# Two layers of modulation, a 31-tap convolution and its norm spread over the engines of one core

## What is computed

```python
cond = silu(c)
mod = cond @ ada_w[l] + ada_b[l]              # l = 0, 1; 1024 x 3072 each
shift, scale, gate = split(mod, 3)
h = rms_norm(x, norm_g[l]) * (1 + scale) + shift
z = h @ even_w_in                             # 1024 x 7296
a_val, a_glu, a_gate, r, k, v, wd, ad, b_gate = split_cols(z)
u = a_val * sigmoid(a_glu)
y = depthwise_conv(u, conv_w, width 31) + conv_vec[0]
ya = silu(layer_norm(y, conv_vec[1], conv_vec[2])) * silu(a_gate)
yb = group_norm(state recurrence of r, k, v, decay, a) ... * silu(b_gate)
x = x + gate * (concat(ya, yb) @ even_w_out)
```

## Time and profile before

| | us |
|---|---|
| median of 3 runs | 2145.01 (2143.09 to 2145.21) |
| the profiled execution: its own time | 2143.33 |
| its span | 2141.6 |
| PE busy | 2029.2 (95%) |
| DVE busy | 1356.5 (63%) |
| ACT busy | 920.6 (43%) |
| POOL busy | 69.5 (3%) |

### The profile page before, as it was taken

The page is one execution under the profiler, slowest core; times in us unless marked ns, Lnnn a source line. Parts: engine busy times, 40 slices in busy tenths (PEclk is TensorE's granted clock), DMA queues, the critical chain, the costliest instruction groups (busy, mean ns, idle before and its releaser), DMA issues. The chain is left out here.

```text
span 2141.6 us, 28761 instructions
## 1 busy us (share of the span) xinstructions
PE 2029.2 (95%) x12095; PEld 1811.2 (85%) x12095; DVE 1356.5 (63%) x1667; ACT 920.6 (43%) x1062; POOL 69.5 (3%) x109
## 2 busy tenths in 40 slices
PE   4987999879999999999999989999999999999998
PEld 3876888667778786899998879999999999998976
DVE  6779758642274223666532358787879787878872
ACT  1511111112125311344433357676767676666654
POOL 2000000000000010000021000000000000000000
PEclk7989899989999999999999999999999999999999
DMA  9834421323332243255674239898989899898980
GB/s 312 282 118 144 151 80 59 120 78 107 131 118 79 79 160 114 64 158 187 191 242 140 100 139 367 313 364 315 359 316 355 320 347 338 330 348 327 353 320 21
DMA packets 225884, 452.22 MB, mean 211 GB/s; under 512 B 6976, under 2 KB 91208, under 8 KB 225752
## 3 DMA queue, kind: packets, MB, share of 16 engines
q1 hardware_dynamic: 222432, 445.44, 59.4%
q0 software_dynamic: 1632, 4.75, 0.8%
q10 hardware_dynamic: 1688, 0.15, 0.1%
HBM read 448.21 MB, written 2.10 MB: 210 GB/s over the span
## 5 line engine op out<-in xcount | busy, mean ns | idle before, releaser
L1726 DVE TENSOR_TENSOR ring_r<-ring,his_r 128x2816 fp32r<-128x2816 f32 (+1 forms) x192 | 587.1, 3087 | 57.6 <-ACT his_r L1337 57.2
L1337 ACT ACTIVATE his_r<-ring 128x2816 fp32r<-128x2816 f32 (+1 forms) x192 | 490.8, 2560 | 194.6 <-DMA ring<-in_moe_w_dram 183.1
L1023 PE MATMUL bank<-his_r,hg_r 128*128 128x352 f32 x2048 | 355.5, 326 | 0.8 <-ACT hg_r L1359 0.8
L1023 PEld LDWEIGHTS bank<-his_r,hg_r 128*128 128x128 f32 x2048 | 332.9, 188 | 2.0 <-issue 0.9
L2183 PE MATMUL bank<-hT,ring 128*128 128x256 f32 x912 | 217.0, 395 | 14.4 <-DVE arena L2726 10.8
L2183 PEld LDWEIGHTS bank<-hT,ring 128*128 128x128 f32 x912 | 176.3, 197 | 43.2 <-issue 18.3
L1023 PE MATMUL bank<-ring_r,hg_r 128*128 128x352 f32 x1024 | 186.1, 324 | 0.0
L1967 PE MATMUL bank<-arena,ring 128*128 128x256 f32 x800 | 178.2, 380 | 1.8 <-ACT cw L1279 0.7
L1967 PEld LDWEIGHTS bank<-arena,ring 128*128 128x128 f32 x800 | 151.4, 190 | 24.4 <-issue 1.3
L1023 PEld LDWEIGHTS bank<-ring_r,hg_r 128*128 128x128 f32 x1024 | 169.2, 188 | 0.0
L1967 PE MATMUL bank<-hT,ring 128*128 128x256 f32 x624 | 142.4, 386 | 5.8 <-ACT hT L2491 4.0
(11 more groups left out here) (492 smaller groups left out, 2541.0 us busy)
## 6 DMA issues: line engine op xcount, KB each, us to landing
ring<-in_moe_w_dram SPq DMA_DIRECT2D x128, 1408.0 KB, 8.1
ring<-in_moe_w_dram SPq DMA_DIRECT2D x48, 1536.0 KB, 8.9
ring<-in_even_w_in_dram SPq DMA_DIRECT2D x28, 1024.0 KB, 6.7
ring<-in_ada_w_dram SPq DMA_DIRECT2D x24, 1024.0 KB, 9.4
ring<-in_ffn_w_dram SPq DMA_DIRECT2D x22, 1024.0 KB, 5.4
ring<-in_odd_w_in_dram SPq DMA_DIRECT2D x9, 2048.0 KB, 7.7
ring<-in_moe_w_dram SPq DMA_DIRECT2D x16, 1024.0 KB, 6.6
ring<-in_a_w_in_dram SPq DMA_DIRECT2D x6, 2048.0 KB, 8.0
```

What stands on the lines that cost most here:

```text
L1023: ins = mm(bank[first + m][:, 0:WC], x[:, KT // 2 * late + k, :], w[:, k, WC * m:WC * m + WC], start=(not late and k == 0 and s == "hg_hi" ...
L1337: A(moe_hi(n), moe_w(n), ACT.Copy).then_inc(sem("moe_hi"), 1)
L1726: V.tensor_tensor(moe_lo(n), moe_w(n), moe_hi(n).bitcast(F32), ALU.subtract).then_inc(sem("moe_lo"), 1)
```

## The change

Five things are edited. **First**, groups 0 and 2 of the modulation go to PE: `ada_direct` takes the raw weight chunk as stationary operand and the column `cond` as moving operand, 32 matmuls of one column a group. DVE keeps the ten other groups. **Second**, the reciprocal of the first norm (L2704) stands between the halves of group 3, `kar(0)` ahead of the second val0 tile, and the DVE steps of zV tiles 0 and 1 in the inversion, at t = 29 and 31. **Third**, channel tiles 3 and 7 of the convolution leave DVE: ACT makes each tap's product (`tap_products`, 31 a tile, three buffers), POOL adds it up (60 additions). DVE keeps 186 taps, all of them done by the second chunk of `states(1)`. **Fourth**, the convolution's layer norm goes into chunks 2 and 3 of `states(1)`. **Fifth**, `eoA` starts right behind `states(1)`, and the head norm's steps stand between its tiles.

```diff
+        TAP_PART = [side[:, 3312 + T * b:3312 + T * b + T] for b in range(3)]
+        TAPS, PRE, LATE_TILES = 186, 29, (3, 7)
...
+        ADA_PE = (0, 2)
+        ADA_DVE = tuple(c for c in range(12) if c not in ADA_PE + ADA_ACT)
+        add("adaP", 4, 512, 2 * len(ADA_PE), 1, ada_src(ADA_PE), reader="ada_pe")
+        add("adaD", 4, 512, 2 * len(ADA_DVE), 1, ada_src(ADA_DVE), reader="dve")
...
             # gpsimd
+            for g, ct in enumerate(LATE_TILES):
+                for j in range(1, 31):
+                    b = 30 * g + j - 1
+                    pool.wait_ge(sem("tap_products"), 31 * g + j + 1)
+                    if b >= 1:
+                        pool.wait_ge(sem("tap_added"), b)
+                    pool.tensor_tensor(YY[:, ct, :], YY[:, ct, :], TAP_PART[b % 3], ALU.add).then_inc(sem("tap_added"), 1)
...
             # tensor
+            def ada_direct(c):
+                n = 2 * ADA_PE.index(c)
+                halves = [wait_chunk(pe, "adaP", n, 0), wait_chunk(pe, "adaP", n + 1, 0)]
+                for j in range(4):
+                    for k in range(KT):
+                        ins = mm(bank[2][:, 4 * c + j:4 * c + j + 1], halves[k // 4][:, k % 4, j * P:(j + 1) * P], cond[:, k:k + 1],
+                                 start=(k == 0), stop=(k == KT - 1))
+                ins.then_inc(sem("ada_columns"), 2)
...
             for q in range(KT):
                 norm_tile(0, q)
-            for c in range(4):
-                ada(c)
+            ada(1)
+            ada_direct(2)
+            ada(3)
...
             z("val0", 0)
-            z("val0", 1)
             pe.wait_ge(sem("rwkv_set"), 3)
             for g in range(8):
                 kar(0, g)
+            z("val0", 1)
...
+                    if tt == 1 and n == 2:
+                        pe_sum(bank[3][:, 0:T], YY, [(taps, TAPS), (sem("tap_added"), 60)], sem("mean_summed"))
+                    elif tt == 1 and n == 3:
+                        pe_sum(bank[2][:, 0:T], YSQ, [(sem("squares_ready"), 9)], sem("var_summed"))
                     fill(n, 0)
...
+            eo(0)
             pe_head_sum(bank[2][0:16, 0:T], YT, [(sem("y_ready"), 4)], sem("head_summed"))
-            pe_sum(bank[3][:, 0:T], YY, [(taps, 248)], sem("mean_summed"))
+            eo(1)
             pe_head_spread(nr[0:16, :], [(sem("gn_mean_ready"), 1)], sem("spread_ready"))
-            pe_head_sum(bank[2][0:16, 0:T], A4T_SQ, [(sem("squares_ready"), 9)], sem("head_summed"))
-            pe_sum(bank[3][:, 0:T], A3T_SQ, [(sem("squares_ready"), 10)], sem("var_summed"))
+            eo(2)
+            eo(3)
+            pe_head_sum(bank[2][0:16, 0:T], A4T_SQ, [(sem("squares_ready"), 10)], sem("head_summed"))
+            eo(4)
             pe_head_spread(nr[0:16, :], [(sem("head_norm"), 2), (sem("centred"), 5)], sem("spread_ready"))
-            for q in range(KT):
-                z("eoA", q, lambda k: YY[:, k, :], (lambda k: (sem("conv_gated"), k // 4 + 1)) if q == 0 else None)
+            for q in range(5, KT):
+                eo(q)
...
             # scalar
+                        b = 30 * g + j - 1
+                        if b >= 3:
+                            act.wait_ge(sem("tap_added"), b - 2)
+                        A(TAP_PART[b % 3], UP[:, ct, j:j + T], ACT.Copy, scale=cw[:, 8 * j + ct:8 * j + ct + 1])\
+                            .then_inc(sem("tap_products"), 1)
...
             for n in range(NC4):
                 carry(0, n)
+                tap_products(3)
+                value(4 + 2 * n) if n < 2 else glu(2 * n)
+                tap_products(3)
+                value(5 + 2 * n) if n < 2 else glu(2 * n + 1)
+                tap_products(2 if n < 3 else 1)
             act.wait_ge(sem("glu_used"), 2)
             b_gate(0)
+            tap_products(3)
             for n in range(8, 12):
                 toks_taken(n)
             b_gate(1)
+            tap_products(3)
             for n in range(12, 16):
                 toks_taken(n)
             for m in range(2, 6):
                 b_gate(m)
+                tap_products(4)
...
             # vector
+            dve.wait_ge(sem("norm_rooted"), 1)
+            step(V.reciprocal(nr[:, :], nr[:, :]))
+            ada(3, 1)
             modulation(0, 0, 16)
...
             for t in range(1, C):
+                if t in (29, 31):
+                    value(t // 31)
...
-            for q in range(KT):
-                lerp(q + 18, "zV", q, VV[:, q, :], col("mu_v", q))
-                if q < 6:
-                    ada(1, 6 + q)
+            for q in range(2, KT):
+                value(q)
+                ada(9 + (q - 2) // 2, q % 2)
...
-            conv(40)
-            states(0, 16)
+            conv(PRE)
+            states(0, lambda n, m: 8)
...
-            states(1, 16)
+            states(1, lambda n, m: (8, 8, 9)[2 * n + m] if 2 * n + m < 3 else 0)
             y_add(1)
-            conv(248)
```

More of the change, by code:

```diff
@@ L282, in z_bank, with ada_group @@
             return bank[ZTILES.index((name, q)) % 2][:, 0:T]
[L284 to L288, removed]
+        SUMMED = {c: sum(b not in ADA_PE for b in range(c + 1)) for c in range(-1, 12)}
+        def ada_group(c):
+            name, groups = next(x for x in (("adaP", ADA_PE), ("adaD", ADA_DVE), ("adaA", ADA_ACT)) if c in x[1])
+            return [(name, 2 * groups.index(c)), (name, 2 * groups.index(c) + 1)]
+        order = [x for c in range(4) for x in ada_group(c)] + [("zL", 0), ("zK", 0), *ada_group(4), ("zK", 1), *ada_group(5), ("zK", 2),
+                                                               *ada_group(6), ("zK", 3), *ada_group(7), ("zR", 0)]
+        a8 = ada_group(8)
+        order += [a8[0], ("zR", 1), a8[1], ("zR", 2), ("zR", 3), ("val0", 0), ("val0", 1), ("glu0", 0), ("glu0", 1), ("zV", 0),
+                  *ada_group(9), ("zV", 1), *ada_group(10), ("zV", 2), *ada_group(11), ("zV", 3)]
         order += [(n, j) for n in ("val1", "glu1", "zB", "zA") for j in range(phases[n]["n"])]
@@ L2610, in b_gate, with tap_products @@
                 evict("zB", m, BG[:, m, :], ACT.Silu).then_inc(acc_taken["act"], 1)
+            tap = [0]
+            def tap_products(n):
+                for m in range(tap[0], tap[0] + n):
+                    g, j = m // 31, m % 31
+                    ct = LATE_TILES[g]
+                    if j == 0:
+                        act.wait_ge(sem("glu_used"), g + 1)
+                        act.wait_ge(sem("inverse_ready"), 1)
+                        act.wait_ge(sem("ada_summed"), SUMMED[11])
+                        A(YY[:, ct, :], UP[:, ct, 0:T], ACT.Identity, bias=col("cv0", ct), scale=cw[:, ct:ct + 1]).then_inc(sem("tap_products"), 1)
+                    else:
+                        b = 30 * g + j - 1
[3 more added lines that the diff above has]
+                            .then_inc(sem("tap_products"), 1)
+                tap[0] += n
             w_taken(0)
@@ L2709, in _ @@
             dve.wait_ge(sem("cond_ready"), 1)
-            for j in range(4):
-                ada(0, j)
+            ada(1, 0)
+            ada(1, 1)
             dve.wait_ge(sem("params_taken"), 1)
@@ L2865, in states, with conv_centre, conv_scale @@
                     V.tensor_tensor(SS[:, :, :], SS[:, :, :], pe_, ALU.mult).then_inc(sem("state_ready"), 1)
-                    conv(fill // 2)
+                    conv(fill(n, 1))
+                    if tt == 1 and n == 3:
+                        conv_scale()
+            def conv_centre():
+                dve.wait_ge(sem("mean_summed"), 1)
+                mean = bank[3][:, 0:T].unsqueeze(1).to_broadcast([P, KT, T])
+                V.scalar_tensor_tensor(YY[:, :, :], mean, -1.0 / D, YY[:, :, :], ALU.mult, ALU.add).then_inc(sem("centred"), 1)
+            def conv_scale():
+                dve.wait_ge(sem("rooted"), 2)
+                step(V.reciprocal(cw[:, :], cw[:, :]))
+                dve.wait_ge(sem("centred"), 1)
+                nrb = cw[:, :].unsqueeze(1).to_broadcast([P, 4, T])
+                for g in range(2):
+                    V.tensor_tensor(YY[:, 4 * g:4 * g + 4, :], YY[:, 4 * g:4 * g + 4, :], nrb, ALU.mult).then_inc(sem("scaled"), 1)
             def y_add(tt):
```

223 lines of the change are left out of this document (124 added, 99 removed).

## The result

| | us |
|---|---|
| before: median | 2143.82 (2142.01 to 2147.40, 20 runs) |
| changed: median | 2147.62 (2143.26 to 2158.69, 20 runs) |
| ratio | 1.0018, 95% interval 1.0009 to 1.0026 |
| span of the profiled execution | 2141.6 before, 2144.3 changed |

The change costs 0.18%, where the forecast was a gain of 0.24%. The time lies outside the 2135 to 2145 that the forecast gave itself; only the wide range of 2131 to 2152 holds it, near the price of rival 1 (2147.3). The sign is the other one.

What follows compares the result with a forecast made beforehand. PE, busy 95% of the span, was taken as the bound, so its idle time, low clock and added work count. −4.2 + 8.5 + 2.7 + 3 − 15.2 = −5.2 gave 2139.8 us; own range 2135 to 2145, wide range 2131 to 2152.

Steps and rivals of the forecast that it cites:

- rival 1: At the start, one-column matmuls leave PE at 1.2 GHz: A +3.3 or +8, time 2147.3 or 2152.0; chance 0.28.
- A: Start up to the first projection: groups 0 and 2 on PE, one-column records taken as warm; −4.2 us.
- B: Middle, zV tiles and inversion: PE and DVE go in lock step around the groups' sums; +8.5 us.
- C: Between the halves: ACT's three tap products ahead of its evictions, twice, lengthen PE's waits; +2.7 us.
- D: Convolution: POOL's additions and DVE's taps don't run at once; +3 us, from 0 to +8.
- E: End, from the states to `eoB`: convolution's norm in the states, head pieces covered by tiles; −15.2 us.
- rival 2: POOL at its bound in the convolution: every overrun lands, D +8, time 2144.8; chance 0.12.
- rival 3: No low clock in the new places: B +4.1, E −18.8, time 2131.8; chance 0.17.
- rival 4: Tail not ready: last taps, additions or gates late, `eo(0)` waits some 6 us; time 2145.8; chance 0.05.

Runs made afterwards that it cites:

- e1: The changed kernel with groups 0 and 2 of the first modulation back on DVE, the reciprocal still between group 3's halves: 2140.22 us, ratio 0.9988 to the kernel before.
- e3: The changed kernel with ACT's three tap products behind the evictions of tokens' matrices 8 to 11 and 12 to 15: 2143.09 us, ratio 1.0012 to the kernel before.
- e5: The changed kernel with useless 256-column matmuls ahead of group 0 and among the one-column ones of both direct groups: 2157.21 us, ratio 1.0060 to the kernel before.
- e6: The changed kernel without POOL's 60 additions, a one-column memset in their place, so taps are missing from the result: one execution, 2139.78 us.
- e8: The changed kernel with the head norm's four steps ahead of all eight tiles of the convolution's product: 2150.90 us, ratio 1.0043 to the kernel before.
- e2: The changed kernel with PE's sums of groups 9 and 10 moved behind zV tiles 5 and 7: 2140.54 us, ratio 0.9991 to the kernel before.
- e4: The changed kernel with the edits of e1, e2 and e3 together: 2131.54 us, ratio 0.9948 to the kernel before.
- e7: e4 with the last chunk of zV's weights loaded ahead of group 11's two chunks: 2125.18 us, ratio 0.9919 to the kernel before.

## Why the prediction was wrong

**A, wrong, and it decides the sign.** The step that failed is "That is why I take warm": the low clock of the one-column blocks was put at nothing. It rested on 32 eight-column records at a clock of 1.00. Group 2 shows that this row couldn't carry it: its first 28 records, too, ran at 1.00 and 0.10 us each, and then the clock fell to 0.50 and stayed there. The row in question had about as many (33) and ended there. Group 0 ran at the low price throughout, 13.78/64 = 0.215 a record, and ended at 29.6 instead of 25. The block of group 2 took 10.53 instead of 7.5 and started at 35.66 instead of 31. So rival 1 came true, between its half and its full form (+3.3, +8): group 0 all cold, as it says, group 2 cold from near the end of its first half on. I had the price, 0.234 a cold record, and the place of the decision, but gave it 0.28. The last sum's own row, cold at 39.32 and 16 records at 26.11 that were warm only behind the 256-column sum of the norm, would have been the better witness for a start from idle.

A second term of A was too small by itself: 1.7 us from DVE's last half (39.5) to the projection (41.2). Before, the sum starts at 39.32 and the projection at 44.80; less the reciprocal that is 3.7, and 2.8 with a sum at the high clock. The changed kernel took 3.7 (46.05 to 49.79). With a warm group 2 DVE's last half, which ended at 43.6, would have set the start to some 46.4 (an estimate: 43.6 and 2.8), so the cold group 0 alone would have turned A's sign. The reciprocal itself was counted rightly, on DVE between its halves; in the changed kernel PE's block hides it, and in e1, where nothing does, it gains nothing.

**B, right in mechanism; the exact size is luck.** PE waits 7.67, 4.10 and 4.11 us ahead of the three sums, and B is +8.5 as forecast in this pair of executions. The same code took 5.8 to 8.7 us more than before in the executions of e1, e3, e5, e6 and e8. What I did not see is the load that stands right behind it (e2, e4), which matters only for the repair.

**C, right in mechanism; the clock was left out.** The waits grew by 1.27 and 1.02, where 1.35 each was forecast. The rest of the 5.6 is the clock, for which the sum had nothing: the tile behind the first turn took 5.30 where 3.6 is usual (granted clock 0.70 from 321 to 325 us; in e8, behind the same wait, 1.00 from 320 to 324), and the spread behind the second 5.08 where 3.7 is. In e5 and e8 the same waits of 2.70 and 1.27 left the clock up, and C was +2.3; in e1, e2 and e6 it was +5.6. So a wait of 2.7 us may or may not bring the low clock with it.

**D, right in mechanism, too large**: 1.8 against 3. The lock is there (e6), but an addition costs DVE 0.4 us where 0.58 was counted, and DVE's idle takes nearly all of it.

**E, right**: −16.3 against −15.2. The order was as forecast, no wait above 1.21 us among the twelve pieces. Of the 3.6 counted for the low clock behind the two spreads, 3.3 were lost, and all at the first (9.93 for two tiles instead of 7.2, and 0.6 in the spread itself).

With A as it was measured and the rest as forecast, the sum would have been +4.0, and 1.0018 is +3.9 us. That they meet is luck: in this pair of executions C came out 2.9 above its forecast, D and E together 2.3 below, and 1.9 came back behind the layer. Rivals 2, 3 and 4 did not happen: the additions found room, the clock did fall in B's waits (1.86 for the first sum, 9.21 for two tiles), and the tail was ready.

## What to carry to other kernels

Work that is moved from a busy engine to an idle TensorE should be priced at the lower clock unless a row shows otherwise: here one-column matmuls neither lifted the clock (group 0) nor held it (group 2), and the sum behind them still cost 1.84 instead of 0.95. On an in-order engine, ask of every moved step what is queued behind its wait. Here two sums over the partitions stood two tiles too early; with both moved back, 8.5 us came back (e2), and another 6.1 when the next load was issued ahead of two that could wait (e7). And a change with five parts is a sum of large terms: with one part taken back, two placed better, one load moved forward and the tail kept, the kernel was 0.8% faster than before, where the change as it stood was 0.2% slower.

## What the runs showed that I had not expected

**The clock column at the start.** Group 0 of the changed kernel ran at the low price while PEclk says 1.00:

```profile
19.00:23.00 4.00, 4.00 (x20) 1.00 1.08 377
```

20 records in 4.0 us is 0.20 each; in e5, where the column says 0.50, it was 1.70/8 = 0.21. The column is not always wrong there: in e5 it says 1.00 over the eight wide matmuls, too, and they did have the high price. So ahead of the first change that the column shows, its 1.00 can stand for either clock in these traces, and the price of a known instruction decides.

**The same wait at several prices.** Far behind the layer, in code that is the same in both, PE waits 2.77 us for DVE, and two tiles follow. Before, then changed:

```profile
829.66 1.23 PE L793 MATMUL bank<-arena 64*128 64x256 f32 x4 [2.77 <-DVE arena L1593]
830.82 9.80 PE L784 MATMUL bank<-hT,ring 128*128 128x256 f32 x32
```

```profile
834.53 1.22 PE L812 MATMUL bank<-arena 64*128 64x256 f32 x4 [2.77 <-DVE arena L1612]
835.68 8.29 PE L803 MATMUL bank<-hT,ring 128*128 128x256 f32 x32
```

The same two tiles cost 9.80 and 8.29: the low clock lasted longer in the one. That is 1.5 of the 1.9 us that the changed kernel regains behind its layer, and no merit of the change. The same holds of whole stretches. These are three of them (us), each only for the executions whose code in it is that of the changed kernel, and the kernel before for comparison:

| stretch | before | changed | e1 | e2 | e3 | e5 | e6 | e8 |
|---|---|---|---|---|---|---|---|---|
| first projection to first chunk of half 0 (B) | 205.2 | 213.6 | 213.8 | | 210.9 | 211.0 | 211.6 | 211.9 |
| tile zB 0 to first matrices of half 1 (C) | 21.8 | 27.4 | 27.4 | 27.4 | | 24.1 | 27.4 | 24.1 |
| `eoB` to the end of the span | 1664.2 | 1662.3 | 1665.6 | 1665.5 | 1666.2 | 1662.2 | 1662.1 | 1661.8 |

So B and C can differ by 3 us each, and the code behind the layer by 4, without any edit. Why the changed kernel's runs spread over 15 us (2143 to 2159) and those of the kernel before over 5 is not settled: there is one profile of each, from the lower half of its runs. A term of one or two microseconds is therefore read from the timeline, wait by wait; the median of a few runs can't tell it, and where the clock has a part in it a single timeline can't either.
